# A hybrid diffusion trunk on one core: Fourier mixer folded by symmetry over channels, and the whole modulation map of layers 1 to 3 as row tiles on VectorE

## The reference

```python
def ada_mods(cond, w, b):                       # w: (1024, 6 * 1024) for each layer
    mod = (jax.nn.silu(cond) @ w + b)[:, None, :]
    return jnp.split(mod, 6, axis=-1)           # shift, scale, gate for the mixer, then for the FFN

def fourier_mix(h, w):
    hg = h.astype(jnp.float32).reshape(B, L, 4, 256)
    f = jnp.fft.fft2(hg, axes=(1, 3), norm='ortho').real
    return f.reshape(B, L, D).astype(h.dtype) @ w

def conv_ffn(h, w_in, conv_w, conv_b, w_out):
    u = h @ w_in
    up = jnp.pad(u, ((0, 0), (1, 1), (0, 0)))
    u = up[:, :-2] * conv_w[0] + up[:, 1:-1] * conv_w[1] + up[:, 2:] * conv_w[2] + conv_b
    gate, val = jnp.split(u, 2, axis=-1)
    return (jax.nn.silu(gate) * val) @ w_out
```

## Time and profile before

| | us |
|---|---|
| median of 3 executions | 2736.66 (2734.59 to 2737.37) |
| the profiled execution | 2735.88 |
| its span in the trace | 2733.9 |
| busy: TensorE, weight loads | 2642.0 (97%), 2422.2 (89%) |
| busy: VectorE, ScalarE, GpSimd | 1926.9 (70%), 1246.6 (46%), 125.2 (5%) |
| mean granted TensorE clock | 0.986 of full |

### The profile page before, as it was taken

The page is one execution under the profiler, slowest core; times in us unless marked ns, Lnnn a source line. Parts: engine busy times, 40 slices in busy tenths (PEclk is TensorE's granted clock), DMA queues, the critical chain, the costliest instruction groups (busy, mean ns, idle before and its releaser), DMA issues.

```text
span 2733.9 us, 43879 instructions
## 1 busy us (share of the span) xinstructions
PE 2642.0 (97%) x16320; PEld 2422.2 (89%) x16320; DVE 1926.9 (70%) x3602; ACT 1246.6 (46%) x2197; POOL 125.2 (5%) x146
## 2 busy tenths in 40 slices
PE   6989999999998999999899999999998999999999
PEld 4966889999998999999779899999997789999998
DVE  3688489758876887698733897588768947754772
ACT  3468354325525552354323553254346936632541
POOL 1000100000012000000101000000100010000000
PEclk9999999999999999999999999999999999999999
DMA  7123233333331424433302333332321012221222
GB/s 285 62 100 137 88 137 108 136 134 112 112 130 63 143 95 149 150 115 123 100 1 71 138 108 136 134 121 104 115 86 44 2 47 70 77 82 65 77 81 81
DMA packets 69329, 281.48 MB, mean 103 GB/s; under 512 B 7984, under 2 KB 10160, under 8 KB 62512
## 3 DMA queue, kind: packets, MB, share of 16 engines
q1 hardware_dynamic: 69168, 279.23, 29.7%
HBM read 276.05 MB, written 3.15 MB: 102 GB/s over the span
## 4 chain that ended last, share of the span: by engine, by line
PE 91%; DVE 6%; ACT 1%; issue 1%; DMA 1%; POOL 0%; SPq 0%; DVEq 0%; ACTq 0%
PE ps L578 20%; PE ps L576 16%; PE ps L577 16%; PE ps L579 15%; PE ps L580 11%; PE ps L795 2%; PE ps L780 2%; PE ps L690 2%; PE ps L894 2%; PE ps L764 1%; PE ps L637 1%; DVE h L1388 1%; DVE prob L1591 1%; PE ps L831 1%; PE ps L572 1%
## 5 line engine op out<-in xcount | busy, mean ns | idle before, releaser
L578 PE MATMUL ps<-h,w_hi 128*128 128x512 f32 x1768 | 700.8, 396 | 0.0
L576 PE MATMUL ps<-h,w_hi 128*128 128x386 f32 x1768 | 607.4, 344 | 9.8 <-DVE h L1388 5.0
L577 PE MATMUL ps<-h,w_hi 128*128 128x386 f32 x1768 | 603.1, 341 | 0.0
L962 ACT ACTIVATE tail<-ps 128x256 f32<-128x256 f32 x281 | 107.6, 383 | 1083.7 <-PE ps L580 1083.7
L579 PE MATMUL ps<-h,w_lo 128*128 128x386 f32 x1768 | 598.9, 339 | 0.0
L580 PE MATMUL ps<-h,w_lo 128*128 128x256 f32 x1768 | 503.2, 285 | 0.0
L580 PEld LDWEIGHTS ps<-h,w_lo 128*128 128x128 f32 x1768 | 333.7, 189 | 79.5
L1264 DVE TENSOR_TENSOR w_lo<-w_raw,w_hi 128x1024 fp32r<-128x1024 f32 (+1 forms) x288 | 378.1, 1313 | 32.3 <-ACT w_hi L957 28.8
L576 PEld LDWEIGHTS ps<-h,w_hi 128*128 128x128 f32 x1768 | 339.3, 192 | 23.1 <-issue 9.9
L957 ACT ACTIVATE w_hi<-w_raw 128x1024 fp32r<-128x1024 f32 (+1 forms) x288 | 323.8, 1124 | 39.9 <-DVE x L1480 21.6
L577 PEld LDWEIGHTS ps<-h,w_hi 128*128 128x128 f32 x1768 | 335.9, 190 | 0.0
(11 more groups left out here) (160 smaller groups left out, 3917.0 us busy)
## 6 DMA issues: line engine op xcount, KB each, us to landing
w_raw<-in_w_in SPq DMA_DIRECT2D x176, 512.0 KB, 3.6
w_raw<-in_w_out SPq DMA_DIRECT2D x64, 704.0 KB, 4.1
ada_w<-in_ada_w SPq DMA_DIRECT2D x42, 1024.0 KB, 5.8
row_w<-in_ada_t SPq DMA_DIRECT2D x48, 512.0 KB, 3.5
w_raw<-in_w_qkv SPq DMA_DIRECT2D x24, 512.0 KB, 3.6
ada_w<-in_ada_t SPq DMA_DIRECT2D x12, 1024.0 KB, 6.3
ada_w<-in_ada_t SPq DMA_DIRECT2D x24, 512.0 KB, 3.5
w_raw<-in_w_o SPq DMA_DIRECT2D x16, 512.0 KB, 3.5
```

The source lines that it names most:

```text
L576: pe.matmul(main, wh, b[:, 0, 0:MAIN], start=first, stop=False)
L577: pe.matmul(main, wh, b[:, 1, 0:MAIN], start=False, stop=False)
L578: pe.matmul(wide, wh, b[:, :, MAIN:NT], start=first, stop=last, skip_group_check=True)
L962: act.activation(tail[par][:], ps[:, 2 * par + 1, TAIL:2 * TAIL], ACT.Copy).then_inc(tail_copied, 1)
```

## The change

1. **Fourier mixer.** The cosine part is even and the sine part odd in the output channel. Stage 1 makes 129 cosine and 128 sine columns (`FCH` = 258 with one spare). Stage 2 makes three results for each group: even (128 rows), odd (128 rows) and the middle channel (1 row). VectorE subtracts and adds even and odd into `folded`, ScalarE copies the middle row over row 0 of the second, and `h_hi` and `h_lo` are made from `folded`. The rows of `w_fnet` are permuted on the host to the mirrored order.
2. **Modulation.** No chunk is left in the layers. Per half there are 10 up rows, then 8 pairs of down rows in the first half and 6 in the second. All down units of the first half and units 0 to 5 of the second have a pair; pairs 6 and 7 of the first half are loaded in up units 0 and 1 of the second.
3. **Gate.** ScalarE makes `f_hi` (`gate_high`) in even up units, and VectorE makes `f_lo` behind it (`gate_low`), except for the last pair of a half. In even units `split_lo` follows `late`.
4. **Loops.** TensorE's up units are a loop in all layers; SyncE's are unrolled in all.

```diff
-PE_CHUNKS = 4
-UP_ROWS = 8
-DOWN_TURNS = 6
+UP_ROWS = 10
+DOWN_PAIRS = (8, 6)
...
             def load_down_rows(j, layer, half):
-                sp.wait_ge(row_used, rows_in(layer, half) + UP_ROWS + max(j - 1, 0) + 1)
-                n = 2 if j < 2 else 1
+                sp.wait_ge(row_used, turns_in(layer, half) + UP_ROWS + max(j - 1, 0) + 1)
+                row = 48 * layer + SECOND_TILE * half + UP_ROWS + 2 * j
+                sp.dma_start(down_row(j % 2), t["ada_t"][row:row + 2].rearrange("a p k -> p a k")
...
+                    for n in range(2 * HALF):
+                        load_units(ub + n, 1)
+                        if more and half and n < 2:
+                            load_down_rows(DOWN_PAIRS[0] - 2 + n, layer, 0)
+                        if more and n % 2 == 0 and 0 < n <= 2 * UP_ROWS:
+                            load_up_row(n // 2 - 1, layer, half)
...
                                 for n, (hx, tab) in enumerate(((h_hi, tab_hi), (h_hi, tab_lo), (h_lo, tab_hi))):
-                                    mm = pe.matmul(ps[:, 4 + tb % 4, :], hx[:, 2 * g + kk, at:at + P],
+                                    mm = pe.matmul(ps[:, 4 + tb % 4, 0:FCH], hx[:, 2 * g + kk, at:at + P],
...
+                        parts = ((0, P, 2), (P, P, 6), (2 * P, 1, 2))
+                        for c, (col, rows, first) in enumerate(parts):
                             for tb in range(4):
+                                for n, (ab, tab) in enumerate(((ab_hi, tab_hi), (ab_hi, tab_lo), (ab_lo, tab_hi))):
+                                    mm = pe.matmul(ps[0:rows, c, :], ab[:, tb, col:col + rows],
+                                                   tab[:, first + tb, :], start=(tb == 0 and n == 0),
+                                                   stop=(tb == 3 and n == 2))
...
-                    if not last:
-                        ada_multiply(batch, 0, 0, chunk_turn(c0))
...
-                    if not last:
-                        ada_turn(batch)
...
+                        act.activation(even_sb[:, LAT0:LAT0 + LAT], ps[:, 0, :], ACT.Copy)
+                        act.activation(even_sb[:, CTX0:CTX0 + CTX], ps[:, 3, 0:P], ACT.Copy).then_inc(even_copied, 1)
                         for c in range(2):
+                            act.wait_ge(folded_made, 2 * g + c + 1)
+                            if c:
+                                act.wait_ge(ft_mm, 8 * g + 8)
+                                act.activation(folded[1][0:1, LAT0:LAT0 + LAT], ps[0:1, 2, :], ACT.Copy)
+                                act.activation(folded[1][0:1, CTX0:CTX0 + CTX], ps[0:1, 3, 2 * P:3 * P],
+                                               ACT.Copy).then_inc(middle_put, 1)
+                                act.wait_ge(middle_put, g + 1)
+                            for at, n, cnd in STREAMS:
+                                op = act.activation(h_hi[:, 2 * g + c, at:at + n], folded[c][:, at:at + n], ACT.Copy)
...
+                    def gate_high(p, i=0):
+                        act.wait_ge(prod_made, i * 2 + (p0 + p + 2))
+                        act.activation(dst, prod[:], ACT.Copy).then_inc(fh_made, 1)
...
+                            for c, op in enumerate((ALU.subtract, ALU.add)):
+                                for at, n, odd in ((LAT0, LAT, ps[:, 1, :]), (CTX0, CTX, ps[:, 3, P:2 * P])):
+                                    made = dve.tensor_tensor(folded[c][:, at:at + n], even_sb[:, at:at + n], odd, op)
+                                made.then_inc(folded_made, 1)
...
                             rescale(i * 4 + (ub + n), n % 2)
-                            split_lo(i * 4 + (ub + n + 2), n % 2, KT)
-                            late(n - 1, i)
-                            if n % 2 and not last:
-                                up_dots(i * 2 + n // 2, layer, half)
+                            if n % 2:
+                                split_lo(i * 4 + (ub + n + 2), n % 2, KT)
+                                late(n - 1, i)
+                                if not last:
+                                    up_dots(i * 2 + n // 2, layer, half)
+                            else:
+                                late(n - 1, i)
+                                split_lo(i * 4 + (ub + n + 2), n % 2, KT)
+                                gate_low(i * 2 + (n // 2 - 1), i * 2 + (p0 + n // 2 - 1), i * 2 + (g0 + n // 2))
...
-                    if not last:
-                        ada_copy(batch, (batch - FIRST_PAIRS) * PE_CHUNKS + NCH)
...
                             update(i * 2 + (ud + 2 + n), n, i * 2 + (2 + n), gate)
                             split_lo(i * 2 + (ud + 4 + n), n, HALF)
                             if not last:
-                                down_dots(i * 2 + (2 + n), n, i + 1, layer, half)
+                                down_pair(i * 2 + (2 + n), n, i + 1, layer, half)
...
                         update(ud + n, n % 2, n, gate, half and n == KT - 1)
                         split_next(ud + n)
+                        if not last and n < DOWN_PAIRS[half]:
+                            down_pair(n, n % 2, n // 2, layer, half)
```

More of the change, by code:

```diff
@@ L39 @@
 NHEADS = 16
+FCH = 258
 FF = 2816
@@ new lines, in _ @@
+                        parts = ((0, P, 2), (P, P, 6), (2 * P, 1, 2))
+                        if g:
+                            pe.wait_ge(even_copied, g)
+                            pe.wait_ge(folded_made, 2 * g)
+                            pe.wait_ge(middle_put, g)
+                        for c, (col, rows, _) in enumerate(parts):
+                            part = P if c == 1 else 0
+                            pe.matmul(ps[0:rows, 3, c * P:(c + 1) * P], ab_ctx[:, col:col + rows],
+                                      ctx_tab[:, part:part + P], start=True, stop=True)
@@ L919, in _ @@
                         unit(ub + 1, 1, KT, h_tiles, None, ub // 2)
[L920 to L933 removed]
+                    with pe.Fori(0, HALF // 2) as i:
+                        for n in range(4):
+                            u = ub + 2 + n
+                            unit(i * 4 + u, n % 2, KT, h_tiles, None, i * 2 + u // 2)
                     def gated(kk):
@@ L1328, in ada_dots @@
+                dve.tensor_tensor(mods[(layer + 1) % 2][:, tiles, :], dots[:], ada_bias[:, layer + 1, tiles, :],
+                                  ALU.add).then_inc(row_put, 1)
             def ada_dots(row, n):
@@ L1714, in _ @@
                     own.leave(HALF // 2 - 1)
-                    for n in range(2 * HALF - 5, 2 * HALF):
+                    for n in range(2 * HALF - 5, 2 * HALF - 1):
                         rescale(ub + n, n % 2)
-                        if n < 2 * HALF - 1:
+                        if n % 2:
                             split_lo(ub + n + 2, n % 2, KT if n + 2 < 2 * HALF else HALF)
-                        late(n - 1)
+                            late(n - 1)
+                            if not last:
+                                up_dots(n // 2, layer, half)
+                        else:
+                            late(n - 1)
+                            split_lo(ub + n + 2, n % 2, KT if n + 2 < 2 * HALF else HALF)
+                            gate_low(n // 2 - 1, p0 + n // 2 - 1, g0 + n // 2)
@@ L1831, in lay_out @@
     ck = i["cache_k"][0].reshape(2, P, 2, P).transpose(0, 3, 2, 1)
+    slot = np.arange(P)
+    mirrored = np.concatenate([np.concatenate([slot, np.where(slot == 0, P, 2 * P - slot)]) + 2 * P * g for g in range(4)])
     out = {
```

204 lines of the change are left out of this document (85 added, 119 removed).

## The result

The changed kernel takes 2717.26 us (median of 4 runs, 2715.93 to 2720.81) against 2735.93 for the kernel before beside it (4 runs, 2734.59 to 2737.37): a ratio of 0.9935, 95% interval 0.9923 to 0.9947. It is faster by 0.65%. The forecast was 2706.8 us, so the sign and the range (2689 to 2719) hold, the likeliest case's own range (2698 to 2714) does not. Of the 29.1 us forecast, the profiled executions show 2733.9 - 2715.1 = 18.8.

What follows compares the result with a forecast made beforehand. TensorE was taken to bound the kernel, carrying 91% of the chain. Chunks and turns 33.1 plus Fourier net 13.3 less backlog 17.25 gave 29.1 us off 2735.9, so 2706.8 us, range 2689 to 2719.

Steps and rivals of the forecast that it cites:

- the likeliest case: Whole kernel: the forecast of 2706.8 us with its own range 2698 to 2714, chance 0.57.
- Chunks and turns: Layers 0 to 2: 24 ada chunks at 1.20 us and 6 row turns at 0.71 leave TensorE's path, 33.1 us less.
- Up stages and half 0: ConvFFN up stages and first-half down stages: added VectorE rows stay hidden, TensorE still sets the pace, cost 0.
- slower rival: Even up units: `split_lo` behind the product ends too late, TensorE waits; 0.8 us per pair gives 2777 us; chance 0.06.
- Backlog of the second half: Looped second-half down units: VectorE needs 11.8 us against 9.73; losses 6.9, 1.75, 8.6 us in layers 0, 1, 2; sum 17.25.
- just in time: Looped down unit n = 4, second half: the split ends 9.4 us after the unit's end, needed at 9.73.
- Fourier mixer: Mixer: fewer matmuls and shorter stages save 17.5 us, less 4.2 for half clock, so 13.3 net.
- 2 x 2.1 = 4.2 us: Mixer: half-clock loss after TensorE idles 4.3 us in each of two groups, taken off the mixer's gain.
- The bound of 2 x 7: Mixer: upper bound on the half-clock loss, two waits at 7 us, half of 14 us; the lower bound was 0.
- the prediction's own sign: Mixer: Fourier groups 17.2 us apart would show it right, groups still 20 us apart wrong; 20.9 before.
- No backlog: Second-half down units: VectorE's pairs fit, losses only 0 to 4.5 us, kernel 2689 to 2694 us; chance 0.2.
- Fourier gains nothing: Mixer: handoffs, with the clock at half for whole groups, take all the gain; kernel 2720 us; chance 0.12.

Runs made afterwards that it cites:

- e2: The changed kernel with the Fourier mixer of the kernel before; rows, gate and loops as changed: 2720.35 us, ratio 0.9949 to the kernel before.
- e5: The changed kernel plus extra matmuls no result uses, 15 in Fourier groups 0 to 2 and 8 before the products with `w_fnet`: 2707.84 us, ratio 0.9900.
- e3: The changed kernel without GpSimd's additions of squares 2 to 5 in the second halves' looped down units: 2707.36 us, ratio 0.9894.
- e4: The changed kernel with ScalarE splitting the next weights before waiting for update and addition in looped down units: 2701.02 us, ratio 0.9868.
- e6: The changed kernel with the edits of e4 and e5 together: 2688.62 us, ratio 0.9829.
- e8: The kernel of e6 plus extra unused matmuls at the starts of layers 1 and 2: 2691.32 us, ratio 0.9832.
- e7: As e5 but with 8 and 4 extra matmuls instead of 15 and 8: 2710.93 us, ratio 0.9912.

## Why the prediction was right or wrong

**Chunks and turns: right.** -33.0 us measured, -33.1 forecast. A difference of periods read from unit starts holds the gaps, and nothing else became the bound in these stages. The 10.4 us between the 29.1 forecast and the 18.7 of the table are 8.7 in the mixer and 2.6 in the backlog, less 1.0 in stretches with no forecast of their own (below).

**Up stages and half 0: right.** The periods stay at 7.05 and 9.73 us. `split_lo` was forecast 5.5 us after the unit's end with 1.5 us to spare; it came at 5.2, with 1.8 left. The slower rival hung on this margin and did not happen.

**Backlog of the second half: right in mechanism, and in size for layers 0 and 2.** 11.8 us per looped unit, TensorE waiting 1.6 to 1.75 us before unit 7, +7.1 (6.9 forecast) at layer 0 and +8.6 (8.6) at layer 2. The agreement at layer 0 is closer than the term deserves: the same edit cost 5.7 us there in e2 and 5.5 in e5, though the last sum started as late; those two had 17.1 us at half around the pooling, after 20.5. Layer 1 cost 4.2 instead of 1.75. About 1.6 of that is clock: the window from 1320 to 1330 was granted 0.83, 3.4 us at half, and in the traces of e2 and e5 the same end has no such stretch and costs 2.7 and 2.6. The remaining 0.9 is of two kinds. Unit 6, forecast "just in time", made TensorE wait 0.33 us and took 10.34 us instead of 9.73, and a wait of 1.65 us made unit 7 longer by 1.9 (11.68 against 9.75 in layer 0).

**Fourier mixer: right in sign and mechanism, mis-sized in the term "2 x 2.1 = 4.2 us" for the half clock.** The forecast was 17.5 gross, 13.3 net; measured 4.6. Of the 8.7 us between them, e5 shows 9.3 - 4.2 = 5.1 to be clock. I had counted two waits of 4.3 us at 2.1 us each. The waits were the right length (4.39 us) and the price of one nearly right (9.3 / 4 = 2.3 us), but there were four: 3.9 us in the first group, 4.4 in the second and third, and 3.1 before the products with `w_fnet`. Behind the first three the half clock fell into stage 2, behind the fourth into the first unit with `w_fnet`. The bound of 2 x 7 held the truth, but only because it priced one wait at three times its cost. By the prediction's own sign, groups still 20 us apart, this part was wrong: they stand 20.4 us apart. The Trainium skill ("TensorE: Matmul & The Clock Gate", HAM oscillation) describes this pattern, a penalty paid again at every tile because each tile ends in a wait, there for a DMA. With the rows of e5 beside it, that is what this mixer did, with waits for VectorE. The other 3.5 us are gross: with the clock kept full, e5 gains 107.35 - 93.37 = 14.0 of 17.5. Its groups stand 18.2 us apart where I forecast 17.2, and its fourth handoff, from 1400.52 to the first matmul of stage 2, takes 5.84 us instead of 4.7. The three small context matmuls, which I had at some 0.3 us, take 0.92 (1372.94 to 1373.86), and they stand between the fifth block and stage 2, on the path, four times. Together that is up to 2.5 us; how the rest divides is open.

**Not forecast.** The start was 4.7 us shorter and the attention of layer 3 with layer 2's first up unit 3.7 us longer. Neither has an edit in it, and it is luck that they nearly cancel. Start and first attention together take 336.7 to 342.3 us over the ten traces of this study; what moves them is open. The 3.7 us go with the clock. Layer 2's first up unit takes 11.7 us in after and e3, with 3.4 us at half in it, and 10.1 in the other eight traces without. Layer 3's attention takes 268.9 to 269.4 us in the five traces with 23.9 us at half in it, after among them, and 267.2 to 268.1 in the five with 17.1, before among them.

**Rivals.** No backlog (2689 to 2694) would have been a reordered line away, as e4 and e6 show, but not in this kernel. "Fourier gains nothing" at 2720 is nearer to the median than my forecast was. Its reason, the half clock for much of a group, was the right one, its size too large: the fold kept 4.6 us in the trace, and 1.1 in the medians when it stands alone.

## What to carry to other kernels

When work is taken off TensorE in a stage that is set by handoffs, count every wait that it leaves there. Several short waits in a row can put a large part of the stage at half clock; here it was a third of the mixer, and it took 9.3 of 14.0 us. When an engine falls behind in a loop, first look at the order of waits on the engine that feeds it: here one split behind a wait cost more than the doubled dot product (16.2 us back against 9.9). And a stretch that another engine bounds gains little from a faster clock, as the layer boundaries of e8 suggest.

## What the runs showed of the hardware that was not expected

A wait of 1.75 us before the last unit of a stage had a half clock behind it in layer 1 of after (granted 0.83 over 1320 to 1330), and waits of 1.65 us at the same place in layers 0 and 2 had none. Waits of 2.25 us in one execution fell on both sides (e7). A matmul with one output row (128x512 into 1 row) is followed by the next after 0.23 us (1405.65 and 1405.88 in after), as one with 128 rows is. At full clock the 512-column matmuls of the mixer started 0.234 us apart (1355.64 to 1363.84 in e5, 35 steps).
